# Constant matmuls in TensorE's gaps before the first product and between the routing steps of a diffusion backbone step

## The reference, cut to what matters

```
mod = silu(cond) @ w_ada + b_ada             -> sh1, sc1, g1, sh2, sc2, g2
h   = rmsnorm(x, g_norm1) * (1 + sc1) + sh1
u   = h @ w_in                               (1024 -> 7168)
mix = merge(conv branch, rg_lru branch, gates of u) @ w_o
x   = x + g1 * mix
h   = rmsnorm(x, g_norm2) * (1 + sc2) + sh2
lg  = h @ w_router_group  + b;   grp = argmax(lg)          (4 groups)
le  = h @ w_router_expert + b;   top 2 of the group's 8    (32 experts)
y   = sum over experts e: gate_e * (silu(h @ w1[e]) * (h @ w3[e])) @ w2[e]
x   = x + g2 * y;   out = rmsnorm(x, g_final)
```

## Time and profile before

| | |
|---|---|
| median of 3 runs | 1086.9 us (1086.29 to 1088.58) |
| the profiled execution's own time | 1089.24 us |
| its span, first to last instruction | 1087.5 us |
| busy, of the span | PE 89%, PEld 65%, DVE 60%, ACT 51%, POOL 29% |
| mean granted TensorE clock | 0.938 of full speed |
| HBM traffic | 300.33 MB moved, 276 GB/s in the mean |

### The profile page before, as it was taken

One profiled execution on the slowest core, in us unless ns is written; L12 is line 12 of the kernel. 1 busy time (PEld: TensorE's weight loads), 2 busy tenths in 40 slices (PEclk: granted clock), 3 DMA queues, 4 the chain that ended last, 5 costly groups with the idle time before them and its releaser, 6 DMA issues.

```text
span 1087.5 us, 12945 instructions
## 1 busy us (share of the span) xinstructions
PE 964.0 (89%) x4226; PEld 709.8 (65%) x4226; DVE 655.4 (60%) x889; ACT 554.9 (51%) x791; POOL 317.5 (29%) x188
## 2 busy tenths in 40 slices
PE   4597979897999899867699999999999999999970
PEld 2396968786899899435466666666656656656640
DVE  2489493447103342156687787787787777777725
ACT  4273626371334231112576676666766766667623
POOL 0235352534455464120333332332332100000002
PEclk9598989898999899977799999999999999999995
DMA  9992253544663430828389999999999999999914
GB/s 348 307 280 100 99 211 124 187 155 155 206 224 113 148 144 20 324 101 328 103 328 404 405 400 403 405 410 387 402 405 403 389 408 397 398 412 400 377 64 174
DMA packets 68399, 300.33 MB, mean 276 GB/s; under 512 B 6474, under 2 KB 17002, under 8 KB 56074
## 3 DMA queue, kind: packets, MB, share of 16 engines
q1 hardware_dynamic: 63674, 286.99, 69.0%
q0 software_dynamic: 3424, 9.08, 2.7%
q10 hardware_dynamic: 1264, 3.76, 0.9%
HBM read 287.75 MB, written 12.07 MB: 276 GB/s over the span
## 4 chain that ended last, share of the span: by engine, by line
PE 65%; DVE 11%; DMA 11%; ACT 7%; SPq 3%; issue 2%; POOL 1%; ACTq 0%; DVEq 0%; POOLq 0%
PE bank L932 16%; PE bank L915 10%; DMA ring<-in_w 9%; PE bank L916 9%; PE bank L792 7%; PE bank L793 7%; PE bank L794 7%; PE bank L905 2%; PE bank L841 2%; SPq L513 2%; DVE lru L1551 1%; DVE lru L1538 1%; ACT lru L1119 1%; PE bank L940 1%; DVE lru L1553 1%
## 5 line engine op out<-in xcount | busy, mean ns | idle before, releaser
L450 POOL TENSOR_TENSOR subs<-ring,subs 128x1024 fp32r<-128x1024 f32 x72 | 180.9, 2519 | 245.1 <-ACT subs L1042 245.1
L932 PE MATMUL bank<-ring,zT_buf 128*128 128x512 f32 x496 | 218.0, 592 | 0.0
L792 PE MATMUL bank<-h_hl,subs 128*128 128x384 f32 x512 | 180.3, 352 | 37.1 <-DVE cp L1573 15.2
L793 PE MATMUL bank<-h_hl,subs 128*128 128x384 f32 x512 | 177.0, 346 | 0.0
L794 PE MATMUL bank<-h_hl,subs 128*128 128x384 f32 x512 | 176.6, 345 | 0.0
L915 PE MATMUL bank<-subs,x_stack 128*128 128x512 f32 x384 | 162.7, 424 | 5.8 <-DVE subs L506 4.2
L932 PEld LDWEIGHTS bank<-ring,zT_buf 128*128 128x128 f32 x496 | 92.0, 190 | 103.9 <-issue 103.8
L916 PE MATMUL bank<-subs,x_stack 128*128 128x512 f32 x384 | 153.2, 399 | 0.0
L506 DVE TENSOR_TENSOR subs<-ring,subs 128x1024 fp32r<-128x1024 f32 x96 | 111.9, 1220 | 47.7 <-ACT subs L1289 47.6
L792 PEld LDWEIGHTS bank<-h_hl,subs 128*128 128x128 f32 x512 | 99.8, 195 | 45.7 <-issue 25.4
L665 POOL DMA_INDIRECT xcy<-h_rows,idx x32 | 109.9, 3435 | 50.8 <-issue 49.1
(11 more groups left out here) (222 smaller groups left out, 1357.5 us busy)
## 6 DMA issues: line engine op xcount, KB each, us to landing
ring<-in_w SPq DMA_DIRECT2D x64, 2048.0 KB, 19.5
gate_w<-in_w SPq DMA_DIRECT2D x16, 2048.0 KB, 24.8
slot<-in_w SPq DMA_DIRECT2D x16, 2048.0 KB, 23.5
ring<-in_w_in SPq DMA_DIRECT2D x14, 2048.0 KB, 7.9
ring<-in_w_ada SPq DMA_DIRECT2D x12, 2048.0 KB, 8.9
expert_rows<-lru SPq DMA_DIRECT2D x27, 160.0 KB
ring<-in_w_rnn_out SPq DMA_DIRECT2D x2, 2048.0 KB, 8.4
ring<-in_w_conv_out SPq DMA_DIRECT2D x2, 2048.0 KB, 8.1
```

Source lines behind the costliest of these rows:

```text
L450: eng.tensor_tensor(pair[:, 1], src, pair[:, 0].bitcast(F32), ALU.subtract).then_inc(done, 1)
L792: eng.matmul(ps[:, 0:T], pair[:, 1, k, :], x[:, 0, k, :], start=(k == 0), stop=False)
L793: eng.matmul(ps[:, 0:T], pair[:, 0, k, :], x[:, 1, k, :], start=False, stop=False)
L932: mm = eng.matmul(bank[4 + half][:, :], zT_buf[:, j * HALF:j * HALF + P], w[:, j, half * 512:(half + 1) * 512], start=(j == 0), stop=(j == ...
```

## The change

A seventh PSUM tensor, `idle_bank` (128x128 f32), takes the products of the two constants. Nothing reads it, and the added matmuls wait for nothing and signal nothing. PE issues 40 of them after `START` and before the first product, and inside the hand-written order 36 after `("wo", 2, 1)`, 4 after `("h2T", 2, 1)`, 24 after `("route", 2)`, 4 after `("rank", 2)` and 44 after `("list",)`.

```
+        idle_bank = ctx.enter_context(nc.psum_tensor("idle_bank", [P, P], F32))
...
+            def keep_running(n):
+
+                for _ in range(n):
+                    eng.matmul(idle_bank[:, :], ones[:, :], ident[:, :], start=True, stop=True)
+
             eng.wait_ge(consts, 6)
             start_work = {"par": transpose_params, "xT": transpose_x, "adaR": ada_rows, "adaC": ada_columns}
             for name, number in START:
                 start_work[name](number)
+            keep_running(40)
             for n, item in enumerate(W_IN):
...
+            KEEP = {("wo", 2, 1): 36, ("h2T", 2, 1): 4, ("route", 2): 24, ("rank", 2): 4, ("list",): 44}
             for name in WO_ON:
                 tile_work[name[0]](*name[1:])
+                keep_running(KEEP.get(name, 0))
```

## The result

The changed kernel takes 1092.71 us (median of 10 runs, 1091.11 to 1095.32) against 1087.93 us (10 runs of the kernel before, 1084.01 to 1090.19). The ratio is 1.0052 with a 95% interval of 1.0036 to 1.0067, which on 1087.9 us is +5.7 us (3.9 to 7.3). The ratio lies near that of the means (1.0052); the two medians alone give 1.0044. It is slower, as forecast, by 4.8 us in the medians against a forecast of 4.2.

A forecast was written before the change was run, and what follows sets the result against it. Prediction: late PE tiles count in the routing's chain of PE, DVE and gather, and the experts' loop has no slack. +4.4 (routing) - 0.2 (first place) = +4.2 us on 1086.9, so 1091.1 us; range 1088.8 to 1095.6, 8 in 10.

The forecast's parts named there:

- third rival: First product: clock rises late or falls again, first full stretch at half speed, +1.5 to +3.1 us, 1092.6 to 1094.3; 14%.
- Price: Each added matmul is two PE instructions of 0.107 us, 0.213 us at full clock and 0.427 at half clock.
- First place: 40 matmuls before the first product: start at half clock, hidden by DVE, last step slightly earlier; -0.3 us, booked -0.2.
- The 36: After the last w_o tile: 7.7 us at full clock, choose 1 starts 3.5 us late, choose 2 +2.7.
- The 24 and the 4: After route 2 and rank 2: the 24 take 5.1 us and just fit, the 4 take 0.85.
- List and the 44: List read +1.6 us; the 44 take 9.4 us, expert 0's transposes start 5.3 later and release ACT 4.4 later.
- The loop: Experts' loop has no slack, so a shift of the first expert shifts the end by as much.
- Faster: Rival: an added matmul costs one instruction of 0.107 us, as a transpose; -3.1 us, 1083.8 us; 5%.
- Dearer: Rival: weight load and stream don't fully overlap, 0.32 to 0.43 us per matmul; 1104 to 1120 us; 5%.
- signs of being right: Among them 304 matmul instructions, route 1 near 504.4, list read near 518.9, transposes behind a fill, second-matrix load near 539 us.
- signs of being wrong: 152 instructions, transpose awaiting gather, first product's last step after 55.1 us, routing clock 0.5, span growing less than load shift.

The follow-up runs named there:

- first_only: The change with only its 40 added matmuls ahead of the first product, none in the routing: 1087.52 us against 1087.78 of the kernel before, ratio 0.9995.
- routing_only: The change with only its 36, 4, 24, 4 and 44 in the routing, none ahead of the first product: 1091.86 us, ratio 1.0050 to the kernel before.
- list_fill_only: The change with only the 44 added matmuls after list, none elsewhere: 1093.27 us, ratio 1.0053 to the kernel before.
- fitted_first60: 16, 3, 22, 4 and 23 added matmuls in the routing and 60 ahead of the first product: 1087.36 us in one run.
- no_list_fill: The change without the 44 after list and without the 40 ahead of the first product: 1089.59 us, ratio 1.0022 to the kernel before.
- wo_fill_only: The change with only the 36 added matmuls after the last w_o tile: 1091.03 us, ratio 1.0030 to the kernel before.
- fitted kernel: The change with routing counts 16, 3, 22, 4 and 23, none ahead of the first product: 1084.34 us against 1087.08 of the kernel before, ratio 0.9974.
- as_transposes: The change with its counts kept, each added matmul a transpose of the same constant: 1087.06 us, ratio 0.9996 to the kernel before.

## Why the prediction was right

Right in the direction, the place and the mechanism; the sum, +4.2 us, was 1.3 us short of the routing distance's 5.5 us. The time alone proves less: 1092.7 us also lies in the third rival's 1092.6 to 1094.3, and only first_only and routing_only exclude it.

- **Price.** Two instructions per product held: 304 matmul instructions for 152 calls. The pace at full clock is 0.112 to 0.113 us in the long fills and not the 0.107 that the earlier trace rows show with 36 columns, so 0.223 to 0.227 per call in place of 0.213. This is the mis-sized term. It adds 0.34 us to the 36, 0.3 to the 24, 0.25 to the two 4 and 0.5 to the 44, some 1.5 us in all. PE has no gap between them, so most of it reaches the transposes: from the start of the 36 they come after 32.5 us (528.12 - 495.59), forecast 31.4 (528.15 - 496.76). The other 0.4 us is taken up by the wait for ACT's copies before route 2 (508.05 to 508.5), which the forecast had and the trace has not. The rest of the 1.3 us is the -0.2 booked for the first place. The Trainium skill ("TensorE: Matmul & The Clock Gate", "Back-to-back issue gap") has about 81 ns per weight load and 128-column matmul, and the estimate from it had 0.32 us per call; the trace agrees with neither, with 0.112 us per pair and 0.223 per call.
- **First place.** Booked -0.2, measured nothing that the runs can tell (first_only, -0.5, from -1.8 to +0.8). That DVE hides the fill held. The step that failed is the assumed start at half clock: in five of the six profiled kernels with a first fill, the change among them, the clock was at 1.00 before it (line 769's last 16 instructions take 1.95 us in place of 3.58). That is no effect of the fill, which comes behind them: list_fill_only, without a first fill, has 1.95 there too. Of the time from half clock to full, 3.0 to 6.2 us in the prediction, fitted_first60 shows 5.2. In the change the fill was over by 44.5 us and the clock fell again in the product. The last step followed DVE's split by 0.05 us in the change (55.52 after 55.47), 0.36 before, with nothing to show for it at the end.
- **The 36.** Choose 1 was forecast 3.5 us late; by the routing distance it is 9.67 - 5.91 = 3.8. Choose 2, forecast +2.7, is 14.81 - 11.90 = 2.9 later.
- **The 24 and the 4.** The forecast let the 24 just fit. They overran by a little: rank 1 starts behind them at 514.68, rank 2 at 515.05, some 0.35 us after DVE's last step for `both_ready` (514.51 + 0.19), and DVE waits 0.25 us for rank 1. Even so no_list_fill against wo_fill_only shows that the 24 and the 4 give 0.7 us back.
- **List and the 44.** The list is read 22.43 - 20.27 = 2.2 us later (forecast 1.6), the transposes start 6.4 us later (5.3), and run at full clock for 0.9 less. The 44 alone, added to the rest, cost 3.5 us.
- **The loop.** That it swallows nothing held over the runs, down to gains: the fitted kernel's -2.75 came out as -2.8.
- **The rivals.** Faster failed on its condition, and as_transposes showed that this was the right condition, yet even there the gain was 0 and not 3.1, since fills that are too short let the clock go. Dearer did not happen. The clock did fall in the first product, as the third rival had it, but rose at 53.7 us, before its last step, and cost nothing that the runs can tell.
- **The signs.** Of the signs of being right, 304 instructions, route 1 at 503.6, the list at 518.3, the transposes behind a fill and the load at 539.22 us came; the clock was 1.00 from 41 us on but for the dip between 50 and 54 us. Two of the signs of being wrong came as well, and neither meant what it was to mean. The first product's last step started at 55.52, later than 55.1, because DVE's own last split ended at 55.47. And the span grew by 1.8 us while that load moved by 4.4, which over many runs is not so (the table above). A sign read as a place in one execution can come for another reason.

## What to carry to other kernels

A fill that keeps PE's clock up is in program order ahead of real work, so its length must be that of the gap, from the pace of the fill's own instructions: count those that the trace shows, not the calls (an f32 product is two). Too long, it holds back the step behind it by the excess, and by more where it starts at half clock (12.6 us against 9.9 for the same 44); too short, the clock is lost all the same. Measure such a change by a distance between two events on either side of it, and read the end time from many runs.

## What the runs showed of the hardware that was not expected

A PE that is busy without a gap need not keep its clock. With 128 moving columns per added product the clock stayed at 1.00 (2.4 GHz) from 495.6 us to the experts. With 36 columns and the same weight loads it fell to 0.50 (1.2 GHz) 5.3 us into the first fill of the routing, 1.1 us into the fill ahead of the first product, and stayed there for some 50 us in the routing, at PE busy 2.00 of 2.00 us. This rests on one execution of the narrow kernel, in which both places show it; what a fill must have to hold the clock was not measured.
